# Gate chunks inside the last head of a differential attention, on one core

## The chip, the cores and the metric

One Trainium2 chip, one core of it. The metric is the device time in microseconds (us) of one execution. The kernel before takes 3123.36 us, the median of three runs (3120.61 to 3126.15).

## The reference

Two blocks one after the other on x of shape 1024 (sequence) x 1024 (channels), f32. The first has a short-convolution layer and a stick-breaking attention, and ends with an RMS norm. The change lies in the second block, which is, shortened:

```
h = rmsnorm_2(x, g_mix)
z = h @ w_in                              # u_pool, q, k, v
y_pool = pool_mixer(u_pool, w_pool_grp, pool_scale)
y_attn = diff_attention(q, k, v, ...)     # 8 heads, two score maps of depth 64 each
gates  = sigmoid(h @ w_gate + b_gate)     # 2048 columns
merged = gates[:, :1024] * (y_pool @ w_branch_pool)
       + gates[:, 1024:] * (y_attn @ w_branch_attn)
x = x + merged @ w_out
x = x + square(relu(rmsnorm_2(x, g_ffn) @ w_up)) @ w_down
```

In `diff_attention` a head's queries and keys are RMS-normalised, biased by distance and softmaxed in two maps; the head's output is (p0 - lambda p1) @ v, RMS-normalised over its 128 columns and scaled.

## The kernel before, in words

Everything is held transposed: channels on the 128 partitions, the 1024 positions along the free axis, in KT = 8 tiles. A **chunk** is one 128-column block of a weight matrix (128 x 1024 f32, 512 KB) times the whole operand: eight **steps**, one for each k tile (`step`, L549, through `mm3`, L541). To keep f32 precision each factor is split in a high part (rounded to fp32r) and a low part (the rest), and a step is three products, high x high, high x low, low x high, over two halves of 512 columns: six matmuls. The operand lies in HH and HL, the weights in WH[2] and WL[2], two slots used in turn.

The 215 chunks are numbered once for the whole program (C_AIN, C_AOUT, ..., C_GA, C_GRP, C_GP, C_QKV2, C_AB, C_WO, C_FF). Each goes through the same relay: SyncE (SP) loads it into the single buffer WR0 when chunk c-1 is fully split (`load_w`, waits on w_lo); ScalarE writes WH when chunk c-2 has been multiplied (`split_w`, L979, waits on chunk_done); GpSimd writes WL = WR0 - WH (L1828, w_lo). So a load, two splits and eight steps follow each other for each chunk, and SP's queue, which takes its instructions strictly in order, sets the order of all transfers.

PSUM is used as four pairs of banks of 1024 columns. Chunks before the second attention use pairs 0 and 1 in turn, by the parity of their number; free[p] counts how often pair p was emptied, and a chunk waits for it. USED gives the count at the start of each stage.

The stages around the change, in order:

- **Gate stage** (C_GA, 8 chunks): h @ w_gate for the attention half. ScalarE evicts each through Sigmoid into T[2] (L1208), SP stores it in g_a in HBM (L478), and ScalarE waits for that store.
- **Group chunk** (C_GRP) and **pool-gate stage** (C_GP, 16 chunks): the pool branch, multiplied by its gates (DVE, L1678), stored in m_p (L484); x is stored in x_d (L486).
- **Differential attention** (C_QKV2, 24 chunks: q, k, v of each head). The head's projections are always made on pair 0. Before the first head, three chunks stand alone. `attention_d` (L854 on TensorE, L1275 on ScalarE, L1712 on DVE) goes through eight slots s for the eight query blocks. Slot s makes the scores of block s (pairs 1 and 2), turns the weights of block s-1 (transposes into bank TB, L866), and for every second block makes the values (`value_sum`, L661, into bank OB). In heads 0 to 6, `steps` puts the 24 steps of the next head's three chunks between them, D_STEPS[s] in slot s, and `group_sums` (L829) adds up squares for the norms of the next queries and keys. DVE subtracts the bias and takes the row minimum (L1703), ScalarE takes exp (L1304, L1307), DVE combines the two maps (L1757, L1392). Each turned group goes PSUM to ATH on ScalarE (L1286) and to ATL on DVE (L1396); the next transposes into TB wait for that.
- **The last head** (j = 7, `fill=False`) has no next projections. The output stage's operand, the eight heads' outputs, is brought back instead: SP loads heads 0 to 5 from y_d into STGab (`operand_back`, L434), heads 6 and 7 are still in dOT. `operand_hi` (L1001, ScalarE) writes HH[k] and `operand_lo` (L1427, DVE) HL[k], one k in each slot from s = 2, and `next_chunk` (L665) gives TensorE one step of chunk C_AB behind it: k = 0 to 4 in slots 3 to 7, k = 5 and 6 behind the last turns. The eighth waits for the norm of the last head's output: copy (L1732), Square (L1345), `output_sums` (L840), Ln and Exp with a table load each (L1246, L1255), `norm_d` (L1389), then `operand_hi` and `operand_lo` for k = 7.
- **Output stage** (C_AB, 8 chunks). The loop over n: DVE multiplies the chunk by its gate, T[n % 2] (L1798), which frees the pair, adds the pool part, T[2 + n % 2] (L1800), and both parts are written to GH and GL. SP, once the last norm is done (d_n), reloads X from x_d (eight loads of 512 KB, L517), then weights, then for each n a gate from g_a (L523) and a pool part from m_p (L524). The T buffers lie over the attention's, so the first gate load also waits until HL is complete (f_lo).
- **C_WO and C_FF**: the projection back and the feed-forward part.

The lines of SP around the end of the last head:

```
            operand_back(y_d, "ab")
            sp.wait_ge(d_n, 3 * KT)
            for k in range(KT):
                sp.dma_start(kt(X, k), x_d[k]).then_inc(ld_xr, 16)
            load_w(C_AB + 2)
            sp.wait_ge(f_lo, FILL["ab"] + KT)
            for n in range(KT):
                if n >= 2:
                    sp.wait_ge(g_lo, KT + n - 1)
                sp.dma_start(T[n % 2], g_a[n]).then_inc(ab_ld[n % 2], 16)
                sp.dma_start(T[2 + n % 2], m_p[n]).then_inc(ab_ld[n % 2], 16)
```

Of the kernel before, what the change touches and what calls it, by code (L numbers as in the profile page):

```python
# [18 lines left out]
F32 = mybir.dt.float32  # L19
# [27 lines left out]
C_GRP = C_GA + KT  # L47
C_GP = C_GRP + 1
C_QKV2 = C_GP + 2 * KT
C_AB = C_QKV2 + 3 * KT  # L50
# [10 lines left out]
for _name, _w in (("mod_b", 64), ("a_g", 8), ("kv_g", 8), ("b_g", 8), ("conv", 24),  # L61
# [16 lines left out]
         ("bout", 4, 4, 0), ("pool", 2, 2, 0), ("ga", 4, 4, 0), ("gp", 8, 8, 0),  # L78
         ("qkv2", 24, 0, 0), ("ab", 4, 4, 0), ("wo", 4, 4, 0), ("ff", 32, 32, 0))
# [51 lines left out]

D_STEPS = (0, 2, 4, 2, 3, 5, 3, 5)
# [20 lines left out]
def block_kernel(nc, xt, cb, vecs, consts, mods, wst, out):  # L153
    with ExitStack() as ctx:
# [76 lines left out]

        raw_at = [[ATT + (2 * n + i) * 4 * S for i in range(2)] for n in (1, 3, 5)]
# [10 lines left out]
        OSUM = (S + HALF, 2 * S + HALF)  # L243
        TB = 3 * S
# [129 lines left out]
        ab_m = sem("ab_m")  # L374
        ff_r = sem("ff_r")
# [9 lines left out]
        def _(sp):  # L385
            def load_w(c):
                sp.wait_ge(w_lo, c)
                sp.dma_start(WR0[:, :], row(wst, c)).then_inc(ld_w, 16)
# [45 lines left out]
            def operand_back(src, name):  # L434
                for k in range(KT - 2):
# [37 lines left out]
            with sp.Fori(0, KT // 2) as i:  # L473
                for m in range(2):
                    s = (C_GA + m) % 2
                    load_w(2 * i + (C_GA + 2 + m))
                    sp.wait_ge(free[s], i + (USED["ga"][s] + 1))
                    sp.dma_start(row(g_a, 2 * i + m), T[2]).then_inc(ga_st, 16)  # L478
            load_w(C_GRP + 2)
            with sp.Fori(0, KT) as n:  # L480
                load_w(2 * n + (C_GP + 2))
                load_w(2 * n + (C_GP + 3))
# [5 lines left out]
            sp.wait_ge(ga_st, 16 * KT)  # L488
# [5 lines left out]
            for c in range(3):  # L494
                load_w(C_QKV2 + 2 + c)
# [5 lines left out]
            def attention_d(j, par, first=False):  # L501
                load_w(3 * j + (C_QKV2 + 5))
                if not first:
                    store_outputs(j - 1, 1 - par, 3 * j + 2)
                load_w(3 * j + (C_QKV2 + 6))
                load_w(3 * j + (C_QKV2 + 7))

            attention_d(0, 0, first=True)
            with sp.Fori(0, (KT - 2) // 2) as i:
                for m in range(2):  # L510
                    attention_d(2 * i + (1 + m), 1 - m)
            sp.wait_ge(d_s, 2 * ST * (KT - 1))
            sp.wait_ge(d_st, 16 * (KT - 2) + 16)
            operand_back(y_d, "ab")
# [25 lines left out]
        def _(pe):  # L540
# [262 lines left out]
            chunks("ga", C_GA, KT, HH, HL)  # L803
# [172 lines left out]
        def _(act):  # L976
# [298 lines left out]
            def attention_d(j, par, fill=True, first=False):  # L1275
# [13 lines left out]
                for s in range(ST):  # L1289
# [6 lines left out]
                    if not late:  # L1296
                        turned(s - 1, 1)
# [694 lines left out]
```

## Time and profile before

| What | Value |
|---|---|
| median of three runs | 3123.36 us |
| the profiled execution, its own time | 3123.29 us |
| its span, first to last instruction | 3121.5 us |
| mean granted TensorE clock | 0.964 |
| busy share of TensorE, DVE, ScalarE, GpSimd | 91%, 41%, 36%, 23% |

A row of the timeline gives the start in us from the span's start, the length in us, the engine (PE is TensorE, ACT is ScalarE, POOL is GpSimd, SPq is SyncE's queue), the line of the code, what is written from what, how often, and in brackets how long the engine stood idle before and what released it. A matmul is pipelined: two of 512 columns in one row last 0.62 us but start 0.46 us before the next two, so distances between starts are what counts. The granted clock is 1.00 at 2.4 GHz and 0.50 at 1.2 GHz.

### The profile page before, as it was taken

To read this page: it belongs to the slowest core of one execution; us is meant where nothing else is said; L and a number is where in the kernel's file an instruction comes from. 1 tells how busy PE (TensorE), PEld (TensorE's weight loads), DVE (VectorE), ACT (ScalarE), POOL (GpSimd) and SP (SyncE) were. 2 spreads that over 40 slices of the span, in tenths; PEclk is the share of its full clock that TensorE was granted. 3 is DMA by queue.
4 is the path that set the end of the run, shared out by engine and by line. 5 is a ranking of instruction groups with operands and counts; after the bars stand their busy time and mean duration, and the time that the engine had idled before them with its cause. 6 is when DMAs were issued, how large, how long until landed. Compare 5 with 4: busy or idle time off the path is not lost.

```text
span 3121.5 us, 38236 instructions
## 1 busy us (share of the span) xinstructions
PE 2855.8 (91%) x13672; PEld 2289.6 (73%) x13672; DVE 1268.7 (41%) x1815; ACT 1128.9 (36%) x1585; POOL 719.7 (23%) x387
## 2 busy tenths in 40 slices
PE   5999998998988875979998999998798999999999
PEld 3888886887777764758786767666586888888887
DVE  5544433125666654361102656556442412112121
ACT  3222213225566553233214666666312312112120
POOL 0222221223444431212232111110121122222222
PEclk8999999999999986989999999999899999999999
DMA  5333311442121120212231000001331111111112
GB/s 198 123 128 112 128 68 54 166 164 95 60 76 54 52 83 10 91 34 87 100 122 64 28 35 27 27 34 61 119 110 47 41 48 51 49 47 47 47 50 98
DMA packets 62571, 236.82 MB, mean 76 GB/s; under 512 B 6944, under 2 KB 7584, under 8 KB 59936
## 3 DMA queue, kind: packets, MB, share of 16 engines
q1 hardware_dynamic: 62496, 235.88, 21.2%
q8 instruction: 40, 0.66, 0.1%
q14 instruction: 35, 0.29, 0.0%
HBM read 191.81 MB, written 44.04 MB: 76 GB/s over the span
## 4 chain that ended last, share of the span: by engine, by line
issue 55%; PE 29%; DVE 6%; POOL 6%; ACT 3%; POOLq 0%; DVEq 0%; ACTq 0%; DMA 0%; SPq 0%
PE PS L545 19%; POOL WL L1828 6%; DVE bC L1581 2%; DVE ATL L1396 2%; PE PS L706 2%; PE PS L728 2%; PE PS L661 2%; ACT PS L1117 1%; PE PS L885 1%; PE PS L691 1%; PE PS L754 1%; PE PS L866 1%; PE PS L711 0%; ACT ATH L1286 0%; ACT bB L1116 0%
## 5 line engine op out<-in xcount | busy, mean ns | idle before, releaser
L1828 POOL TENSOR_TENSOR WL<-WR,WH 128x1024 fp32r<-128x1024 f32 x215 | 521.0, 2423 | 2085.6 <-ACT WH L984 1954.9
L545 PE MATMUL PS<-HH,WH 128*128 128x512 f32 x2272 | 727.6, 402 | 91.4 <-issue 28.9
L545 PE MATMUL PS<-HL,WH 128*128 128x512 f32 x2272 | 714.5, 396 | 0.0
L545 PE MATMUL PS<-HH,WL 128*128 128x512 f32 x2272 | 712.1, 395 | 0.0
L545 PEld LDWEIGHTS PS<-HH,WH 128*128 128x128 f32 x2272 | 426.9, 192 | 196.3 <-issue 72.9
L545 PEld LDWEIGHTS PS<-HL,WH 128*128 128x128 f32 x2272 | 435.7, 192 | 93.8
L545 PEld LDWEIGHTS PS<-HH,WL 128*128 128x128 f32 x2272 | 435.2, 192 | 93.5
L984 ACT ACTIVATE WH<-WR 128x1024 fp32r<-128x1024 f32 x214 | 225.7, 1055 | 589.6 <-PE PS L545 413.1
L545 PE MATMUL PS<-GH,WH 128*128 128x512 f32 x768 | 236.6, 389 | 1.5 <-DVE TMP L1798 1.5
L545 PE MATMUL PS<-GL,WH 128*128 128x512 f32 x768 | 236.5, 389 | 0.0
L545 PE MATMUL PS<-GH,WL 128*128 128x512 f32 x768 | 236.4, 389 | 0.0
L1581 DVE TENSOR_TENSOR_SCAN bC<-PS,EPSC 128x256 f32<-128x256 f32 (+7 forms) x128 | 172.9, 1352 | 102.6 <-ACT PS L1117 102.4
L1856 POOL TENSOR_TENSOR bB<-bB,bC 128x256 f32<-128x256 f32 (+7 forms) x128 | 154.0, 1205 | 177.0 <-DVE bC L1581 175.9
L1396 DVE TENSOR_TENSOR ATL<-PS,ATH 128x512 fp32r<-128x512 f32 (+3 forms) x288 | 152.6, 546 | 50.4 <-ACT ATH L1286 25.9
L545 PEld LDWEIGHTS PS<-GH,WH 128*128 128x128 f32 x768 | 144.0, 188 | 32.1 <-issue 1.9
L545 PEld LDWEIGHTS PS<-GH,WL 128*128 128x128 f32 x768 | 144.2, 188 | 30.0
L545 PEld LDWEIGHTS PS<-GL,WH 128*128 128x128 f32 x768 | 144.2, 188 | 29.9
L1820 DVE TENSOR_TENSOR X<-PS,X 128x1024 f32 x32 | 39.2, 1225 | 292.2 <-PE PS L545 292.2
L691 PE MATMUL PS<-IDF,bB 128*128 128x128 f32 x576 | 99.0, 298 | 58.1 <-DVE ATL L1396 57.4
L691 PEld LDWEIGHTS PS<-IDF,bB 128*128 128x128 f32 x576 | 67.2, 148 | 82.8 <-DVE ATL L1396 52.8
L1811 DVE SCALAR_TENSOR_TENSOR TMP<-PS,TMP 128x1024 f32<-128x1024 f32 x32 | 39.2, 1225 | 208.2 <-ACT TMP L1375 208.2
L1375 ACT ACTIVATE TMP<-PS 128x1024 f32<-128x1024 f32 x32 | 32.9, 1029 | 233.8 <-PE PS L545 233.8
(227 smaller groups left out, 3528.7 us busy)
## 6 DMA issues: line engine op xcount, KB each, us to landing
WR<-wst SPq DMA_DIRECT2D x215, 512.0 KB, 3.4
TMP<-mods SPq DMA_DIRECT2D x48, 512.0 KB, 3.5
MRAW<-mods SPq DMA_DIRECT2D x16, 512.0 KB, 11.0
v_hl<-VS SPq DMA_DIRECT2D x8, 1024.0 KB, 6.3
bV<-v_hl SPq DMA_DIRECT2D x8, 1024.0 KB, 7.6
X<-xt SPq DMA_DIRECT2D x4, 1024.0 KB, 8.1
x_b<-X SPq DMA_DIRECT2D x8, 512.0 KB, 4.8
k_hi<-KSH SPq DMA_DIRECT2D x8, 512.0 KB, 4.8
```

The source lines that it names most:

```text
L545: last = pe.matmul(PS[:, dst0 + q:dst0 + q + HALF], l, rr[:, k * S + q:k * S + q + HALF], start=a, stop=z)
L661: last = pe.matmul(PS[:, OB + (2 * n + r) * P:OB + (2 * n + 2) * P], v[:, kb * P:(kb + 1) * P], a[:, (2 * kb + r) * P:(2 * kb + 2) * P], s ...
L691: last = pe.transpose(PS[:, base + n * P:base + (n + 1) * P], bB[t % 2][h][:, kb * P:(kb + 1) * P], IDF[:, :])
L706: pe.matmul(PS[:, base + c0:base + c0 + w], l[par][rows, q], rr[par][rows, c0:c0 + w], start=i == 0, stop=i == 2 and c0 + w < n)
L728: last = pe.matmul(PS[:, o + r * P:o + 2 * P], value_weights(V, kb, h), a[:, (2 * kb + r) * P:(2 * kb + 2) * P], start=i == 0 and a is ATH ...
L984: act.activation(WH[slot][:, :], WR0[:, :], ACT.Identity).then_inc(w_hi, 1)
L1396: return dve.tensor_tensor(dst, value, high.bitcast(F32), ALU.subtract)
L1581: dve.tensor_tensor_scan(bC[h][:, S - n:S][:, ::-1], c, EPSC[:, 0:1].broadcast_to([P, n]), 1.0, ALU.mult, ALU.bypass).then_inc(free[1 + h], 1)
L1811: dve.scalar_tensor_tensor(out=T[2 + m], in0=PAIR[s], scalar=0.0, in1=T[m], op0=ALU.max, op1=ALU.mult).then_inc(free[s], 1)
L1820: dve.tensor_tensor(x, PAIR[s], x, ALU.add).then_inc(free[s], 1)
L1828: pool.tensor_tensor(WL[slot][:, :], WR0[:, :], WH[slot][:, :].bitcast(F32), ALU.subtract).then_inc(w_lo, 1)
L1856: pool.tensor_tensor(b, b, bC[h][:, S - n + 1:S + 1], ALU.mult).then_inc(b_a, 1)
```

## The change

Three of the eight gate chunks (C_GA2, GA_LATE = 3) leave the gate stage and come behind C_QKV2 in the numbering. The 24 steps are made in the last head, in the order D_LAST (steps ahead of and behind the second turn of each slot), on pair 0, as the projections are in the other heads. ScalarE evicts each without the sigmoid into a staging buffer GAS (`stage_gate`), SP stores it in g_a, and the sigmoid is taken in the output stage when the gate is back, for n = 5, 6, 7. The weights' order in HBM stays; `load_moved` maps the new numbers to the old places. HH and HL hold h until the 24 steps are done, so the operand of the output stage is written behind them: k = 0 ahead of the last turns, k = 1 behind them, 2 to 4 behind the Square, 5 and 6 behind Exp, all on DVE ahead of the last norm, then k = 7. TensorE makes both first output chunks step by step behind the last values, with the output sums after the third step, in pair 2 (OSUM_LAST). The gate stage's loops of SP and ScalarE are written out. On SP the weights of C_AB and C_AB+1 are loaded between the stores of the late gates, and those of C_AB+2 now ahead of the reloads of X.

The diff, cut to its core:

```diff
 C_GA = C_POOL + 4
-C_GRP = C_GA + KT
+GA_LATE = 3
+GA_FIRST = KT - GA_LATE
+C_GRP = C_GA + GA_FIRST
...
-C_AB = C_QKV2 + 3 * KT
+C_GA2 = C_QKV2 + 3 * KT
+C_AB = C_GA2 + GA_LATE
...
+D_LAST = ((0, 0), (2, 0), (2, 3), (0, 2), (2, 0), (2, 1), (2, 4), (2, 2))
...
+        GAS = [nc.alloc_sbuf_tensor_at(f"GAS{i}", [P, S], F32, offset=ATT + (8 + 2 * i) * 4 * S) for i in range(2)]
+        OSUM_LAST = (2 * S, 2 * S + HALF)
...
@@ SP, gate stage @@
+            for n in range(GA_FIRST):
+                s = (C_GA + n) % 2
+                load_moved(C_GA + 2 + n)
+                sp.wait_ge(free[s], n // 2 + (USED["ga"][s] + 1))
+                sp.dma_start(g_a[n], T[2]).then_inc(ga_st, 16)
...
@@ SP, last head @@
+            load_moved(C_GA2 + 2)
             sp.wait_ge(d_s, 2 * ST * (KT - 1))
             sp.wait_ge(d_st, 16 * (KT - 2) + 16)
-            operand_back(y_d, "ab")
+            operand_back(y_d, "ab", 0, 4)
+            for n in range(GA_LATE):
+                if n < 2:
+                    load_moved(C_AB + n)
+                sp.wait_ge(free[0], USED["ab"][0] - GA_LATE + n + 1)
+                sp.dma_start(g_a[GA_FIRST + n], GAS[n % 2][:, :]).then_inc(ga_late[n % 2], 16)
+            operand_back(y_d, "ab", 4)
+            load_w(C_AB + 2)
             sp.wait_ge(d_n, 3 * KT)
             for k in range(KT):
                 sp.dma_start(kt(X, k), x_d[k]).then_inc(ld_xr, 16)
-            load_w(C_AB + 2)
             sp.wait_ge(f_lo, FILL["ab"] + KT)
+            sp.wait_ge(ga_late[0], 32)
+            sp.wait_ge(ga_late[1], 16)
...
@@ TensorE, attention_d @@
                     early = 0 if s in (4, 6) else (D_STEPS[s] + 1) // 2
+                    late = D_STEPS[s] - early
+                    if not fill:
+                        early, late = D_LAST[s]
                     steps(early)
-                    if not fill and s >= 3:
-                        next_chunk(C_AB, C_AB % 2, "ab", s - 3)
                     turn(s - 1, 1)
                     values(s - 1)
-                    steps(D_STEPS[s] - early)
+                    steps(late)
                 if fill:
                     return
                 turn(ST - 1, 0)
-                next_chunk(C_AB, C_AB % 2, "ab", ST - 3)
                 turn(ST - 1, 1)
-                next_chunk(C_AB, C_AB % 2, "ab", ST - 2)
                 values(ST - 1)
                 pe.wait_ge(d_max, 2 * ST * KT)
-                output_sums(3 * KT)
+                pe.wait_ge(free[0], USED["ab"][0])
+                for kb in range(KT):
+                    if kb == 2:
+                        output_sums(3 * KT, OSUM_LAST)
+                    pe.wait_ge(f_lo, FILL["ab"] + kb + 1)
+                    step(C_AB, C_AB % 2, 0, HH, HL, kb)
+                    if 1 <= kb <= 5:
+                        step(C_AB + 1, (C_AB + 1) % 2, 1, HH, HL, kb - 1)
+                for kb in range(5, KT):
+                    step(C_AB + 1, (C_AB + 1) % 2, 1, HH, HL, kb)
...
@@ ScalarE, last head @@
+            def stage_gate(n):
+                act.wait_ge(chunk_done, C_GA2 + n + 2)
+                if n == 2:
+                    act.wait_ge(ga_late[0], 16)
+                act.activation(GAS[n % 2][:, :], PAIR[0], ACT.Identity).then_inc(free[0], 1)
...
                     if not late:
                         turned(s - 1, 1)
+                    if not fill and s == 3:
+                        stage_gate(0)
+                    if not fill and s == 6:
+                        stage_gate(1)
+                        split_w(C_AB, C_AB % 2)
...
                     if not fill:
-                        if s >= 2:
-                            operand_hi("ab", s - 2, dOT)
-                        if s == ST - 1:
-                            operand_hi("ab", KT - 2, dOT)
+                        if s == 3:
+                            split_w(C_GA2 + 2, (C_GA2 + 2) % 2)
                         continue
...
                 if not fill:
+                    stage_gate(2)
+                    operand_hi("ab", 0, dOT)
+                    split_w(C_AB + 1, (C_AB + 1) % 2)
                     turned(ST - 1, 0)
                     turned(ST - 1, 1)
+                    operand_hi("ab", 1, dOT)
                     act.wait_ge(d_o, ST // 2 * KT)
                     act.wait_ge(d_rs, 3 * KT - 1)
                     act.activation(dSQ[:, :], dOT[par][:, :], ACT.Square).then_inc(d_sq, 1)
-                    ln_outputs(3 * KT)
+                    for k in range(2, 5):
+                        operand_hi("ab", k, dOT)
+                    ln_outputs(3 * KT, OSUM_LAST)
                     exp_d(3 * KT, d_lo, KT)
+                    for k in range(5, KT - 1):
+                        operand_hi("ab", k, dOT)
                     act.wait_ge(d_n, 3 * KT)
                     operand_hi("ab", KT - 1, dOT)
...
@@ ScalarE, output stage @@
                     split_w(c + 2, c % 2)
+                if n >= GA_FIRST:
+                    act.wait_ge(ab_ld[n % 2], 32 * (n // 2 + 1))
+                    act.activation(T[n % 2], T[n % 2], ACT.Sigmoid, bias=vec("b_gate", 8 + n)).then_inc(ab_sg, 1)
                 act.wait_ge(ab_m, n + 1)
...
@@ DVE, last head @@
-                        if s >= 2:
-                            operand_lo("ab", s - 2, dOT)
-                        if s == ST - 1:
-                            operand_lo("ab", KT - 2, dOT)
                         continue
...
                 if not fill:
+                    operand_lo("ab", 0, dOT)
                     turned(ST - 1, 0)
                     turned(ST - 1, 1)
+                    operand_lo("ab", 1, dOT)
                     outputs(ST - 1)
+                    for k in range(2, KT - 1):
+                        operand_lo("ab", k, dOT)
                     norm_d(dOT[par], GS8[:, 0:1], 3 * KT)
                     operand_lo("ab", KT - 1, dOT)
...
@@ DVE, output stage @@
                 dve.wait_ge(ab_ld[n % 2], 32 * (n // 2 + 1))
+                if n >= GA_FIRST:
+                    dve.wait_ge(ab_sg, n - GA_FIRST + 1)
                 dve.tensor_tensor(gate, PAIR[s], gate, ALU.mult).then_inc(free[s], 1)
```

## Rows read from the trace of the kernel before

**Rows 1.** The page, part 1: busy us, share of the span, instructions.
```profile
PE 2855.8 (91%) x13672; PEld 2289.6 (73%) x13672; DVE 1268.7 (41%) x1815; ACT 1128.9 (36%) x1585; POOL 719.7 (23%) x387
```

**Rows 2.** Stretches: length, busy us per engine, granted clock, DMA share, GB/s.
```profile
2087.30:2153.80 66.50, 61.64 (x334) 45.87 (x334) 40.60 (x102) 43.87 (x69) 9.85 (x4) 1.00 0.18 63
2153.80:2161.40 7.60, 5.68 (x47) 4.96 (x46) 2.97 (x12) 3.90 (x8) 0.00 (x0) 1.00 0.01 2
2153.80:2229.10 75.30, 47.82 (x259) 35.06 (x258) 47.73 (x110) 41.90 (x69) 0.24 (x1) 0.86 0.06 20
2208.30:2214.30 6.00, 5.96 (x18) 4.69 (x19) 3.23 (x4) 1.20 (x2) 0.00 (x0) 0.50 0.00 0
2229.10:2235.00 5.90, 5.85 (x14) 4.59 (x15) 0.00 (x0) 0.00 (x0) 2.22 (x1) 0.50 0.93 358
```

**Rows 3.** Timeline, TensorE: start, us, instruction, xcount, idle before, releaser.
```profile
2208.34 1.08 PE L866 MATMUL PS<-IDF,dP 128*128 128x128 f32 x4 [2.57 <-DVE ATL L1396]
...
2229.15 1.22 PE L545 MATMUL PS<-HH,WH 128*128 128x512 f32 x2 [7.39 <-DVE HL L1396]
...
2246.14 0.70 PE L545 MATMUL PS<-HH,WH 128*128 128x512 f32 x2 [1.69 <-DVE TMP L1798]
```

**Rows 4.** Timeline, ScalarE, tail of the last head.
```profile
2221.80 1.27 ACT L1246 ACTIVATE dSQ<-PS,EPSC 128x512 f32<-128x512 f32 x2 [0.83 <-PE PS L844]
2223.08 1.28 ACT L1255 ACT_TABLE_LOAD   x1
2224.37 1.06 ACT L1255 ACTIVATE dRS<-dSQ 128x1024 f32<-128x1024 f32 x1
2226.78 1.06 ACT L1007 ACTIVATE HH<-dOT 128x1024 fp32r<-128x1024 f32 x1 [1.35 <-DVE dOT L1389]
2227.74 1.04 ACT L984 ACTIVATE WH<-WR 128x1024 fp32r<-128x1024 f32 x1
```

**Rows 5.** Timeline, DVE, tail of the last head and output stage.
```profile
2225.46 1.28 DVE L1389 SCALAR_TENSOR_TENSOR dOT<-dOT,GS,dRS 128x1024 f32<-128x1024 f32 x1 [6.89 <-ACT dRS L1255]
...
2244.67 1.23 DVE L1798 TENSOR_TENSOR TMP<-PS,TMP 128x1024 f32<-128x1024 f32 x1 [15.58 <-DMA TMP<-m_p]
...
2302.12 3.43 DVE L1800 TENSOR_TENSOR TMP<-TMP,TMP 128x1024 f32<-128x1024 f32 x1
```

**Rows 6.** DMA, 2226 to 2245 (40 slices; then landing us); last, m_p at 2246.
```profile
GB/s 0 0 0 69 155 423 397 423 414 371 173 267 336 397 371 354 354 405 423 423 423 414 448 388 397 397 405 431 423 423 414 414 414 431 328 173 69 26 9 0
...
X<-x_d SPq DMA_DIRECT2D x8, 512.0 KB, 7.4
...
TMP<-m_p SPq DMA_DIRECT2D x1, 512.0 KB, 12.3
...
DMA to landing us min/median/max: 5.5/5.5/5.5
```

**Rows 7.** Timeline, ScalarE, gate stage.
```profile
1457.64 1.28 ACT L984 ACT_TABLE_LOAD   x1 [8.79 <-PE PS L545]
...
1490.30 1.06 ACT L984 ACTIVATE WH<-WR 128x1024 fp32r<-128x1024 f32 x1 [6.11 <-PE PS L545]
```

**Rows 8.** Timeline, handover to the head's projections: TensorE, then ScalarE.
```profile
1640.37 0.73 PE L545 MATMUL PS<-HH,WH 128*128 128x512 f32 x2 [1.32 <-DVE TMP L1678]
...
1649.97 1.06 ACT L984 ACTIVATE WH<-WR 128x1024 fp32r<-128x1024 f32 x1 [0.41 <-DVE NLAM L1689]
```

**Rows 9.** Timeline, TensorE, head 6.
```profile
2115.00 1.98 PE L829 MATMUL PS<-dSQ,dBD 128*128 128x512 f32 x4 [0.26 <-ACT dSQ L1236]
...
2117.16 0.39 PE L661 MATMUL PS<-ATH,dVH 128*128 128x256 f32 x1 [0.18 <-DVE ATL L1396]
...
2119.05 0.70 PE L545 MATMUL PS<-HH,WH 128*128 128x512 f32 x2 [0.22 <-ACT dSQ L1241]
...
2134.24 1.98 PE L829 MATMUL PS<-dSQ,dBD 128*128 128x512 f32 x4
...
2136.64 0.44 PE L866 MATMUL PS<-IDF,dP 128*128 128x128 f32 x2 [0.41 <-DVE ATL L1396]
```

More of the change, by code:

```diff
@@ L374, in block_kernel @@
         ab_m = sem("ab_m")
+        ab_sg = sem("ab_sg")
+        ga_late = [sem(f"ga_late{i}") for i in range(2)]
         ff_r = sem("ff_r")
@@ L385, in _, with load_w, load_moved @@
         def _(sp):
[L386 removed]
+            def load_w(c, at=None):
                 sp.wait_ge(w_lo, c)
[L388 removed]
+                sp.dma_start(WR0[:, :], row(wst, c if at is None else at)).then_inc(ld_w, 16)
+            def load_moved(c):
+                if isinstance(c, int) and C_GA2 <= c < C_AB:
+                    load_w(c, c - C_GA2 + C_GA + GA_FIRST)
+                elif isinstance(c, int) and (c < C_GRP or c >= C_AB):
+                    load_w(c)
+                else:
+                    load_w(c, c + GA_LATE)
             sp.dma_start(CB, cb).then_inc(ld_cb, 16)
@@ L433, in _, with operand_back @@
             sp.wait_ge(st_x, KT * 16)
-            def operand_back(src, name):
-                for k in range(KT - 2):
+            def operand_back(src, name, first=0, last=KT - 2):
+                for k in range(first, last):
                     if k >= 4:
@@ L472, in _ @@
                 load_w(c + (C_POOL + 2))
[L473 to L479, printed above, removed]
+            for n in range(GA_FIRST):
[3 more added lines that the diff above has]
+                sp.dma_start(g_a[n], T[2]).then_inc(ga_st, 16)
+            load_moved(C_GRP + 2)
             with sp.Fori(0, KT) as n:
-                load_w(2 * n + (C_GP + 2))
-                load_w(2 * n + (C_GP + 3))
+                load_moved(2 * n + (C_GP + 2))
+                load_moved(2 * n + (C_GP + 3))
                 sp.wait_ge(free[(C_GP + 1) % 2], n + (USED["gp"][(C_GP + 1) % 2] + 1))
@@ L802, in _ @@
                 chunk(C_POOL + g, s, s, uu[s] + 1)
-            chunks("ga", C_GA, KT, HH, HL)
+            chunks("ga", C_GA, GA_FIRST, HH, HL)
+            chunk(C_GRP - 1, (C_GRP - 1) % 2, (C_GRP - 1) % 2, GA_FIRST // 2 + USED["ga"][(C_GRP - 1) % 2])
             cg = C_GRP
@@ L906, in steps @@
                     nonlocal k
-                    for _ in range(n if fill else 0):
+                    for _ in range(n):
                         c = k // KT
@@ L1202, in _ @@
                 act.activation(kt(MXH, g), T[3], ACT.Identity).then_inc(p_mh, 1)
-            with act.Fori(0, KT // 2) as i:
-                for m in range(2):
-                    s = (C_GA + m) % 2
-                    act.wait_ge(chunk_done, 2 * i + (C_GA + m + 2))
-                    split_w(2 * i + (C_GA + m + 2), s)
-                    act.activation(T[2], PAIR[s], ACT.Sigmoid, bias=vec("b_gate", 2 * i + (8 + m))).then_inc(free[s], 1)
-                    act.wait_ge(ga_st, 32 * i + 16 * (m + 1))
+            for n in range(GA_FIRST):
+                s = (C_GA + n) % 2
+                act.wait_ge(chunk_done, C_GA + n + 2)
+                split_w(C_GA + n + 2, s)
+                act.activation(T[2], PAIR[s], ACT.Sigmoid, bias=vec("b_gate", 8 + n)).then_inc(free[s], 1)
+                act.wait_ge(ga_st, 16 * (n + 1))
             for g in range(4):
```

35 lines of the change are left out of this document (16 added, 19 removed).

## The prediction

> **What bounds the kernel now.** I read the page first: TensorE is busy in 91% of the span [rows 1], so a change pays only where TensorE waits, or where it moves work into a wait. Then the stretches around the last head [rows 2]. In each, the reader compares PE busy with the length, and reads the granted clock. Head 6 (they count from 0), from its first score to the first score of the last, takes 66.5 us, 61.6 of them busy, at clock 1.00: 24 matmul steps of the next head's projections fill it. The last head has only seven steps of the output stage's first chunk: 75.3 us to the eighth, 47.8 busy, clock 0.86. Against a chain of softmax work that 24 steps hardly lengthen elsewhere, some 27 us are idle, and this is the room for the change.
>
> What ends the head's waits is in [rows 3 to 5]. The eighth step starts at 2229.15 after 7.39 us for the last low part, behind the chain Ln, table load, Exp, norm, high part, low part. The first output-stage chunk that needs a PSUM pair back starts at 2246.14: it waits 1.69 us for the multiply at 2244.67, which itself waited 15.58 us for m_p. That load is late because eight reloads of X, 512 KB each, and one weight load stand ahead of it on SP's queue [rows 6]; the first may start only when the norm of the last output is done (2225.46 + 1.28 = 2226.74). m_p needed 12.3 us to land, against 5.5 with little ahead of it. So **two clocks run to 2246**: TensorE's, and norm plus 17.9 us of loads (2244.67 - 2226.74). They are nearly even now.
>
> I count from A, the last head's first score (2153.80, the end of head 6 in its stretch in [rows 2]). Before, the norm is done at A+72.9 and the third output chunk starts at A+92.3.
>
> **Removed ahead of the head: -32.7.** ScalarE takes up a gate chunk when TensorE has finished it; from 1457.64 to 1490.30 are three chunks of 10.9 us with no wait of TensorE between [rows 7]. Three go: 32.7 us. With them goes what each issued: a weight load, a split on ScalarE and one on GpSimd, a sigmoid, a store; all come back later. The group chunk behind the gates now waits for the last eviction at its first product instead of its second. The next wait is for that gate's store either way, so I take 0.
>
> **Handover to the head's projections: -0.6.** Three fewer chunks swap the pairs of the stage before. The 1.32 us wait at 1640.37 for the multiply to free pair 0 disappears, since the multiply now uses pair 1. But ScalarE's next split (1649.97) waits for the lambda chain, which stays [rows 8]. Bounds 0 and 1.3; half, as the split and not the chunk sets the next sum.
>
> **The last head, TensorE to the end of step 24: T = A+62.0.** It now carries 24 steps, as head 6 does, so I start from 66.5. Gone are two group sums of the projections, with what waits on them: 0.26 + 2.16 (2115.00 to 2117.16) + 0.18 and 0.22 around the values, and 2.40 (2134.24 to 2136.64): 5.2 [rows 9]. Gone is the next head's first score, 0.5. New are waits where the single pair 0 changes hands inside a slot. After the eighth step ScalarE must evict (1.06) before the ninth starts: +1.2. The second eviction hides behind the values. The third falls behind the head. The evictions stand ahead of the exponentials of slots 3 and 6, and delay them 1 and 2 us. DVE, the last turns and TensorE wait for those; but head 6 has table loads and a Ln at about those places (1.28 + 1.1 + 1.28 by the like in [rows 4]), and no turn is late there. The low parts of the operand, one for each slot, leave DVE. Sum 66.5 - 5.2 - 0.5 + 1.2 = 62.0. Bounds 60 and 66: below if the values' waits go too, above if the last turn, tied with step 24 (DVE's chain alone gives A+61.8 or so), comes late.
>
> **Behind T: the norm at T+26.1.** From a head's last turn to the end of its values takes 7.60 - 0.5 = 7.1 us [rows 2]. Here ScalarE does the third eviction, a high part and the split of the second output chunk first, 0.96 us apart each [rows 4]; 0.7 us of waiting is in the 7.1 already: +2.2. Two waits of TensorE, about 4 and 1.5 us, should take the clock to 1.2 GHz, as the 2.57 us before 2208.34 and the wait ahead of it did (0.50 for 6.0 us [rows 2, 3]): +2.3 on the values; 0 if it holds. So values end at T+11.6. Three steps follow (4.1, +0.4 for the clock), then the output sums, 1.9: T+18.0. Ln, table load, Exp up to the norm take 3.66 (2221.80 to 2225.46 [rows 4, 5]): T+21.7. But ScalarE and DVE have been given the parts 5 and 6 ahead of the norm: two high parts 1.9, the last low part 1.2, norm 1.3: T+26.1. The switch from Ln to Exp costs 1.28 in the row, with Exp 0.01 us behind it. The Trainium skill (ScalarE: Activation LUTs, What ACT_TABLE_LOAD costs) adds a drain of about 1.38 us to every switch. By it the forecast would be 1.4 us later; the row shows no drain and decides.
>
> **The third output chunk: A+106.3, against A+92.3.** The load of its weights now goes ahead of X's, so 512 KB less are queued: 0.524 MB at 423 GB/s is 1.2 us [rows 6]. Norm to multiply is 17.9 - 1.2 = 16.7, then 1.5 to TensorE's start. 62.0 + 26.1 + 16.7 + 1.5 = 106.3. TensorE is ready at T+12.0 (values, and the slow rest) + 16 steps of 1.36 (a chunk's 10.9 over eight) + 1.3 for the sums = T+35.1 = A+97.1. **So the expected gain of the fill is partly given back in a wait of 9.2 us for the gate loads.** Behind it the clock is down for 5.9 us, as at 2229.1 [rows 2]: 2.9 more. Head and handover cost 14.0 + 2.9 = +16.9.
>
> **Later gates: 0.** Chunks 5 to 7 take their sigmoid in the output stage. Their multiply comes some 2 us later, 3.4 once with a table load; but the add behind it took 3.43 us at 2302.12, against 1.23 for an operation of the same size at 2244.67 [rows 5]; it ran beside GpSimd's split, and a later one need not. TensorE wants the pair a chunk of 10.9 us later. The last sigmoid can run before its chunk ends, once the loads are there. Bound +1.5, if it can't.
>
> **Sum.** -32.7 - 0.6 + 16.9 = -16.4. The profiled execution took 3123.29 us (span 3121.5), the median is 3123.36, so they are the same to 0.1: **3107 us**. The case's own range is 3101 to 3113: no fall of the clock ahead of the values takes 2.3 off, T ends -2 and +4, the last gate +1.5.
>
> **Rivals.**
> - *The gate loads don't wait for X's.* They are issued about 4.4 us behind the norm and land 5.5 later, as the second m_p did [rows 6]. The multiply is at A+98.1, the chunk at A+99.6, the wait 2.5 us: 3123.3 - 33.3 + 7.3 = 3097; 3094 if the clock holds too. Against it: the first m_p took 12.3 us with the same loads ahead. The Trainium skill (DMA: Bandwidth & Descriptors, Queues, rings and completion order) says a later transfer may finish before an earlier one, though rings are consumed in order; by that this rival has its chance, and the trace does not show it.
> - *Half hidden.* The last head's chain takes the evictions and splits badly, T comes 10 to 22 us late, and the time is within 6 us of before.
> - *In series: slower.* Place: the softmax chain of slots 3 to 7, where TensorE reaches a turn only after steps that sit behind ScalarE's evictions. Before, the last turn started at A+54.5, with five steps ahead of it, 8.4 us of that (one at half clock: 2.7 + 4 x 1.4). If all 24 came on top: 46.1 + 32.8 = A+78.9 at full clock, over A+100 with most at 1.2 GHz. It decides from T = A+84.7 on (16.4 + 6.3 later), so with at least four steps at half clock; with all of them slow, about 3150. Against it: head 6 hides the same 24.
>
> **How the numbers follow.** What a measurement of this kernel can tell from no change is 0.2%, or 6.2 us. Forecast 0.75, loads free 0.13, half hidden 0.07, in series 0.05. The first two are faster: 0.88; same 0.07; slower 0.05. The range reaches to the loads rival's low end and past the forecast's high one: 3093 to 3114.
>
> **What would show it.** In the profile of the changed kernel: five sigmoids in the gate stage, and the head's first score 33 us earlier; 24 steps to A+62 at clock near 1.00; about 4 us of waiting between the last two turns; the norm at A+88; after the second output chunk a wait of 9 us that ends on the multiply, and that on m_p, with clock 0.50 behind it. I am wrong if the multiply comes within 3 us of the second chunk's end, if a turn in the head waits over 2 us, or if the output stage's later chunks wait for sigmoids.

## The result and the profile after

The changed kernel takes **3104.2 us** (median of five runs, 3103.5 to 3112.4) against 3122.3 of the kernel before beside it (five runs, 3120.6 to 3126.2): ratio 0.9947, with an interval of 0.9933 to 0.9962, so 18.1 us less by the medians. (The ratio comes from the single runs, so it isn't quite the quotient of the medians.) Two executions among the runs below, one of 5719.6 us in r1 and one of 13154.6 us of the kernel before beside r9, lie far outside all others and are in none of the figures given. The forecast was 3107. The profiled execution took 3104.21 us, its span is 3102.4; with 3123.29 of the one before, the two traces differ by 19.1 us, and it is this sum that they have to explain.

The page, part 1, of the changed kernel, beside [rows 1]:

```profile
PE 2848.9 (92%) x13672; PEld 2286.0 (74%) x13672; DVE 1265.2 (41%) x1815; ACT 1123.1 (36%) x1582; POOL 720.9 (23%) x387
```

The matmuls are the same 13672. TensorE was idle for 3121.5 - 2855.8 = 265.7 us before and is for 3102.4 - 2848.9 = 253.5 now. The rest, 6.9 us, is in the busy time itself, which depends on the clock.

Stretches of the changed kernel, columns as in [rows 2]: head 6; the last head to the end of its 24 steps; its last values; the wait of the third output chunk; what follows it; the start of C_WO; and the whole from A (now 2115.03) to that chunk:

```profile
2048.50:2115.00 66.50, 61.63 (x333) 45.85 (x332) 40.62 (x102) 43.84 (x69) 9.84 (x4) 1.00 0.09 32
2115.00:2177.20 62.20, 57.31 (x325) 44.47 (x325) 36.60 (x98) 30.79 (x57) 7.28 (x3) 1.00 0.23 77
2181.70:2187.50 5.80, 4.29 (x21) 4.09 (x22) 1.92 (x2) 1.54 (x2) 1.15 (x1) 0.57 0.46 142
2213.00:2221.00 8.00, 0.00 (x0) 0.00 (x0) 1.35 (x2) 0.00 (x0) 0.00 (x0) 0.73 1.03 420
2221.10:2226.90 5.80, 5.80 (x14) 4.54 (x15) 4.64 (x4) 2.00 (x2) 2.46 (x1) 0.50 0.15 61
2291.60:2297.60 6.00, 6.00 (x20) 4.76 (x21) 3.09 (x3) 2.00 (x2) 2.50 (x1) 0.72 0.00 0
2115.00:2221.10 106.10, 87.66 (x458) 69.32 (x457) 50.59 (x112) 48.55 (x76) 12.11 (x5) 0.95 0.35 126
```

The same stretch of the kernel before, from A to its last turn:

```profile
2153.80:2208.34 54.54, 36.10 (x212) 26.30 (x211) 41.38 (x104) 32.76 (x59) 0.00 (x0) 0.90 0.06 20
```

The last head now looks like head 6: 57 of 62 us busy at clock 1.00 up to its last turn, where it was 36 of 55 at 0.90. The fourth row of the changed kernel is the price: 8 us in which TensorE does nothing while the DMA engines move 420 GB/s.

TensorE's timeline, beside [rows 3]: the pair handed over inside slot 3, the two last turns, the values, the third output chunk, and the first chunk of C_WO:

```profile
2141.77 0.73 PE L572 MATMUL PS<-HH,WH 128*128 128x512 f32 x2 [1.11 <-ACT GAS L1312]
...
2177.22 0.60 PE L894 MATMUL PS<-IDF,dP 128*128 128x128 f32 x4
2181.69 0.63 PE L894 MATMUL PS<-IDF,dP 128*128 128x128 f32 x4 [3.87 <-DVE ATL L1447]
2183.82 0.55 PE L688 MATMUL PS<-ATH,dVH 128*128 128x256 f32 x1 [1.50 <-DVE ATL L1447]
...
2221.08 1.19 PE L572 MATMUL PS<-HH,WH 128*128 128x512 f32 x2 [8.18 <-DVE TMP L1851]
...
2291.56 1.05 PE L572 MATMUL PS<-GH,WH 128*128 128x512 f32 x2 [2.20 <-DVE TMP L1851]
```

DVE, beside [rows 5]: the last norm, the first gate, the last gate:

```profile
2202.11 1.28 DVE L1440 SCALAR_TENSOR_TENSOR dOT<-dOT,GS,dRS 128x1024 f32<-128x1024 f32 x1
...
2219.61 1.22 DVE L1851 TENSOR_TENSOR TMP<-PS,TMP 128x1024 f32<-128x1024 f32 x1 [13.87 <-DMA TMP<-m_p]
...
2290.07 1.23 DVE L1851 TENSOR_TENSOR TMP<-PS,TMP 128x1024 f32<-128x1024 f32 x1 [4.40 <-ACT TMP L1412]
```

ScalarE, beside [rows 4, 7]: its take-up at the gate stage's end, which was at 1490.30; the last gate's eviction, a high part, a weight split and, behind these three, the eviction of the last turns' first half; Ln's result, table load and Exp; and the last sigmoid:

```profile
1456.37 1.06 ACT L1017 ACTIVATE WH<-WR 128x1024 fp32r<-128x1024 f32 x1 [8.81 <-PE PS L572]
...
2177.42 1.02 ACT L1312 ACTIVATE GAS<-PS 128x1024 f32<-128x1024 f32 x1 [2.28 <-PE PS L572]
2178.34 1.05 ACT L1040 ACTIVATE HH<-STGab 128x1024 fp32r<-128x1024 f32 x1
2179.28 1.05 ACT L1017 ACTIVATE WH<-WR 128x1024 fp32r<-128x1024 f32 x1
2180.23 0.59 ACT L1325 ACTIVATE ATH<-PS 128x512 fp32r<-128x512 f32 x1
...
2196.50 1.28 ACT L1287 ACT_TABLE_LOAD   x1
2197.79 1.06 ACT L1287 ACTIVATE dRS<-dSQ 128x1024 f32<-128x1024 f32 x1
...
2288.78 1.15 ACT L1412 ACTIVATE TMP<-TMP,VEC 128x1024 f32<-128x1024 f32 x1 [4.38 <-DMA TMP<-m_p]
```

And the transfers issued from 2203 to 2222, beside [rows 6] (KB each, median us from issue to landing; g_a and m_p are two loads each, and the first of them took 10.7 and 11.2):

```profile
X<-x_d SPq DMA_DIRECT2D x8, 512.0 KB, 7.5
TMP<-g_a SPq DMA_DIRECT2D x2, 512.0 KB, 9.9
TMP<-m_p SPq DMA_DIRECT2D x2, 512.0 KB, 10.6
```

### The profile page after: what moved, and what is told of

It reads as the page before. It is cut to its first block, busy times and chain, and to the rows that moved or that the text cites. A ratio compares the mean times of both kernels' runs of the same rounds, so it can differ in the third digit from the quotient of the medians.

```text
span 3102.4 us, 38102 instructions
## 1 busy us (share of the span) xinstructions
PE 2848.9 (92%) x13672; PEld 2286.0 (74%) x13672; DVE 1265.2 (41%) x1815; ACT 1123.1 (36%) x1582; POOL 720.9 (23%) x387
## 4 chain that ended last, share of the span: by engine, by line
issue 56%; PE 27%; DVE 6%; POOL 6%; ACT 3%; POOLq 0%; DMA 0%; DVEq 0%; ACTq 0%; SPq 0%
PE PS L572 17%; POOL WL L1881 6%; DVE bC L1632 2%; DVE ATL L1447 2%; PE PS L733 2%; PE PS L755 2%; PE PS L688 2%; ACT PS L1150 1%; PE PS L913 1%; PE PS L718 1%; PE PS L781 1%; PE PS L894 1%; PE PS L738 0%; ACT ATH L1325 0%; ACT bB L1149 0%
## 5 line engine op out<-in xcount | busy, mean ns | idle before, releaser
L572 PEld LDWEIGHTS PS<-HL,WH 128*128 128x128 f32 x2272 | 434.4, 191 | 93.3
```

What stands on the lines that cost most here:

```text
L572: last = pe.matmul(PS[:, dst0 + q:dst0 + q + HALF], l, rr[:, k * S + q:k * S + q + HALF], start=a, stop=z)
```

## The experiments

All were run in three batches on three chips, each with runs of the kernel before beside it (medians 3123.9, 3123.5 and 3124.1 us over 17, 17 and 16 runs; r12 was run alone on a fourth, beside 3126.4). Marks are counted from A, the last head's first score. In that count the changed kernel has: last turn 62.2, norm done 88.4, third output chunk 106.1 after a wait of 8.2.

**r1, the changed kernel again**, for its marks on another chip.

> The changed kernel once more, as the measure for the other runs beside it. 3104 us, within 4. If the 1.2 us by which its profile was ahead of the one before already at 1338 us, where the code is the same, is a matter of the single execution, the two profiles there differ by another amount in this run.

Measured: 3100.1 (the median of four runs, 3094.9 to 3105.2), ratio 0.9917 [0.9902, 0.9931]. Last turn at 62.2, norm at 88.4, third chunk at 105.5 after 7.6. So the marks inside the head and tail repeat to 0.6 us, and the whole time doesn't: it spreads over 10 us. The last section comes back to that. At 1338 us, where the code is the same, this profile is 0.5 us ahead of the one before, and not 1.2: over all the traces here the sums at that place start between 1332.2 and 1339.5. The 1.2 us are a matter of the single execution.

**r2, the first gate loads ahead of X's.** Nothing else is changed:

```diff
             load_w(C_AB + 2)
+            sp.wait_ge(f_lo, FILL["ab"] + KT - 2)
+            sp.dma_start(T[0], g_a[0]).then_inc(ab_ld[0], 16)
+            sp.dma_start(T[2], m_p[0]).then_inc(ab_ld[0], 16)
             sp.wait_ge(d_n, 3 * KT)
...
-                sp.dma_start(T[n % 2], g_a[n]).then_inc(ab_ld[n % 2], 16)
-                sp.dma_start(T[2 + n % 2], m_p[n]).then_inc(ab_ld[n % 2], 16)
+                if n:
+                    sp.dma_start(T[n % 2], g_a[n]).then_inc(ab_ld[n % 2], 16)
+                    sp.dma_start(T[2 + n % 2], m_p[n]).then_inc(ab_ld[n % 2], 16)
```

> The first gate and pool part are loaded ahead of the eight reloads of X, as soon as six low parts of the operand are written. Theory (queue): the 8.2 us wait of TensorE ahead of the third output chunk is for loads that stand behind 4 MB of X; it goes to under 1 us, the third chunk starts at A+98 instead of A+106.1, the clock stays at 1.00 behind it (2.9 us more), total 11 us less than the changed kernel, about 3093. Rival (bandwidth or order only moved): the second gate's loads come behind X instead, TensorE waits ahead of the fourth chunk, and under 4 us are gained: 3100 to 3104.

Measured: **3093.6** (3090.7 to 3096.4), ratio 0.9901 [0.9887, 0.9915]. The stretch from 2190 to 2214 of this kernel, then its DVE in the timeline (A is 2116.41):

```profile
2190.00:2214.00 24.00, 24.00 (x104) 19.16 (x104) 12.93 (x10) 12.82 (x13) 2.39 (x1) 1.00 0.51 187
```

```profile
2209.73 1.22 DVE L1855 TENSOR_TENSOR TMP<-PS,TMP 128x1024 f32<-128x1024 f32 x1 [3.12 <-PE PS L576]
...
2221.69 1.22 DVE L1855 TENSOR_TENSOR TMP<-PS,TMP 128x1024 f32<-128x1024 f32 x1 [4.91 <-DMA TMP<-m_p]
```

TensorE runs through, 24.00 of 24.00 us at clock 1.00, and the first gate's multiply waits for TensorE, at A+93.3 and not at A+104.6. The second one does wait for its m_p, but its chunk is long enough to cover that. From A to C_WO it is 164.7 us against 176.5: 11.8 less, of which the wait is 8.2 and the clock behind it 2.9, as forecast. Against r1's trace (174.5) it is 9.8 less. So the queue was the cause, and the wait costs 10 to 12 us in all in the traces. The times say it less sharply: 10.6 us below the changed kernel, but 6.5 below r1 beside it, and r2's interval overlaps r1's.

**r3, the last turns ahead of most of that work**: on ScalarE the first of them ahead of the gate's eviction and both ahead of the high part and the weight split, and on DVE both ahead of the first low part (ScalarE's part of the edit):

```diff
-                    stage_gate(2)
-                    operand_hi("ab", 0, dOT)
-                    split_w(C_AB + 1, (C_AB + 1) % 2)
                     turned(ST - 1, 0)
+                    stage_gate(2)
                     turned(ST - 1, 1)
+                    operand_hi("ab", 0, dOT)
+                    split_w(C_AB + 1, (C_AB + 1) % 2)
                     operand_hi("ab", 1, dOT)
```

> ScalarE takes the evictions of the last turns ahead of the last gate's eviction, the first high part and the weight split. Theory (what stands ahead on ScalarE, and the clock that falls for it): the 3.87 us wait between the last two turns goes to under 1 us, the values run at clock 1.00 and end at T+7.4 instead of T+11.8, the norm comes at T+21.7 instead of T+26.2, the third output chunk 4.5 us earlier: about 3099.5. Rival (the wait is the bank's, for DVE's low part, and the clock falls in any case): under 1.5 us gained, 3103.

Measured: 3102.1 (3099.0 to 3104.8), ratio 0.9928 [0.9915, 0.9941]. TensorE's timeline and the stretch of the values:

```profile
2181.63 0.63 PE L894 MATMUL PS<-IDF,dP 128*128 128x128 f32 x4 [1.50 <-DVE ATL L1447]
2183.76 0.55 PE L688 MATMUL PS<-ATH,dVH 128*128 128x256 f32 x1 [1.50 <-DVE ATL L1447]
```

```profile
2183.76:2188.80 5.04, 5.04 (x24) 5.04 (x24) 3.88 (x2) 1.96 (x3) 2.47 (x1) 0.50 0.30 106
```

The first wait falls from 3.87 to 1.50, so the work put ahead of the last turns was its cause, and the norm comes 2.0 us earlier. Most of that is ScalarE's three operations, though the run moved DVE's low part too: in the changed kernel DVE was done with it at 2180.65, and still waited 0.20 us for ScalarE. But the values still run at clock 0.50 behind two waits of 1.50: the clock term, which I had tied to the long wait, isn't won back. The third chunk comes only 0.9 to 1.5 us earlier (A+104.6), and the time isn't below r1's. The wait's half of this expectation held, the clock's and the time's didn't.

**r4, the new tail without the fill**: all eight gate chunks back in the gate stage, the last head empty, the output stage's operand still written behind it.

```diff
-GA_LATE = 3
+GA_LATE = 0
-D_LAST = ((0, 0), (2, 0), (2, 3), (0, 2), (2, 0), (2, 1), (2, 4), (2, 2))
+D_LAST = ((0, 0),) * 8
```

> All eight gate chunks back in the gate stage, no steps in the last head, the rest of the new tail kept. Theory (the steps fill waits): without 24 steps the last head's chain still takes 44 to 50 us to its last turn instead of 62, so 12 to 18 of the 32.7 us come back: 3104 + 32.7 - 15 = 3122, 3118 to 3126. Rival (in series): the last turn comes at A+30, the gain of the gate stage and the length of the head cancel: 3104 within 3.

Measured: 3129.1 (twelve runs, 3120.0 to 3133.1), ratio 1.0014 [1.0005, 1.0022]. The last head of this kernel, from A to its last turn, and its third output chunk:

```profile
2152.97:2209.21 56.24, 35.10 (x182) 25.69 (x181) 36.33 (x99) 27.88 (x54) 2.39 (x1) 0.72 0.00 1
```

```profile
2251.42 1.19 PE L564 MATMUL PS<-HH,WH 128*128 128x512 f32 x2 [8.39 <-DVE TMP L1833]
```

This splits the change in two. Writing the operand behind the head costs by itself: the third chunk stands at A+98.4 and not at A+92.3, 6.1 us later, and the whole is 5.3 us slower than before. The 24 steps then lengthen A to the third chunk from 98.4 to 105.5 or 106.1, by 7.1 to 7.6 us, and relieve the gate stage of 32.7: 25 to 26 us net, and 3129.1 less the changed kernel's 3104.2 or r1's 3100.1 is 25 or 29.

The expectation missed: 3129.1 lies above its 3118 to 3126. My number for the head was wrong. Empty, it takes 56.2 us to the last turn, at clock 0.72; the kernel before, with five steps in it, takes 54.5, at 0.90. So a head without the steps is no shorter, and taking their time off, as I did here and in the prediction's "in series" rival (54.5 - 8.4 = 46.1), was the error.

**r5, the last norm two operations earlier** on DVE:

```diff
-                    for k in range(2, KT - 1):
+                    for k in range(2, 5):
                         operand_lo("ab", k, dOT)
                     norm_d(dOT[par], GS8[:, 0:1], 3 * KT)
-                    operand_lo("ab", KT - 1, dOT)
+                    for k in range(5, KT):
+                        operand_lo("ab", k, dOT)
```

> DVE makes the last norm ahead of the low parts 5 and 6. Theory (two clocks: the third output chunk starts norm plus 17.9 us of loads): the norm comes 3.3 us earlier (2202.1 minus 2198.8 in the changed kernel's profile), X's reloads, the gate's load and the third chunk as well: 3101, with a wait of 5 instead of 8.2 us. Rival (the loads are bound by the last low part or by the weights, not by the norm): no change, 3104.

Measured: 3098.4 (3096.7 to 3099.7), ratio 0.9919 [0.9906, 0.9932]. The third chunk in the timeline (A is 2112.19):

```profile
2214.69 1.19 PE L572 MATMUL PS<-HH,WH 128*128 128x512 f32 x2 [4.58 <-DVE TMP L1852]
```

The norm is 3.2 us earlier (85.2), the chunk 3.0 to 3.6 (102.5 against 105.5 and 106.1). So the run of loads that starts with the norm is what counts here, and an operation ahead of the norm moves the third chunk by its length. In the times it isn't to be seen: the ratio is r1's.

**r6, the kernel before with its first gate loads ahead of X's**, the edit of r2.

> The kernel before with the first gate's loads ahead of X's. Theory (in the kernel before the loads and TensorE were nearly even, so the same repair brings only the 1.69 us wait): 1 to 2.5 us less than before, 3120 to 3121. Rival (the loads cost both kernels alike): 8 us or more less, 3114.

Measured: 3122.8, ratio 0.9999 [0.9991, 1.0008]: nothing. Two rows, TensorE and ScalarE:

```profile
2245.97 0.70 PE L550 MATMUL PS<-HH,WH 128*128 128x512 f32 x2 [1.56 <-POOL WL L1833]
```

```profile
2242.32 1.06 ACT L989 ACTIVATE WH<-WR 128x1024 fp32r<-128x1024 f32 x1 [13.40 <-DMA WR<-wst]
```

I had expected 1 to 2.5 us, and that missed. The multiply comes at A+78.6, 12 us earlier than before, and the third chunk at A+92.33, as before (A+92.34). In the kernel before, the chunk's weights also stand behind X. Their low part was ready at 2245.72 (GpSimd, 2243.35 + 2.37), 0.2 us ahead of the gate's multiply (2244.67 + 1.23), so it took over as the last wait. Only the changed kernel loads the weights ahead of X, and only there is the gate load alone last.

**r7, the edits of r2, r3 and r5 together; r8, these and one step moved** from slot 3 to slot 4; **r9, r7 with a semaphore of its own for the g_a loads**, so that the late sigmoid doesn't wait for m_p too; **r11, r7 again.** The edit of r9:

```diff
-                    act.wait_ge(ab_ld[n % 2], 32 * (n // 2 + 1))
+                    act.wait_ge(ab_ga[n % 2], 16 * (n // 2 + 1))
                     act.activation(T[n % 2], T[n % 2], ACT.Sigmoid, bias=vec("b_gate", 8 + n)).then_inc(ab_sg, 1)
```

> Loads first, norm first and turns first together. Theory: with the loads first the norm no longer sets the third chunk, so the sum is 11 from the loads and 4.4 from the turns and their clock, and nothing from the norm: 3104 - 15.4 = 3089. Rival (the parts cover each other, the last low part of the operand becomes the bound): 3093, no better than the loads alone.

> As the one with all three, and the ninth step moved from slot 3 to slot 4, so that the first gate's eviction lies under the scores. Theory: the 1.11 us wait for pair 0 goes, and the last turn comes 1.1 us earlier: 3088. Rival (the last turn is tied with DVE's chain of the last slot, so a step earlier brings nothing): 3089.

> All three repairs, and the gates' loads count on a semaphore of their own, so that the late sigmoids wait for the gate alone and not for the pool part behind it. Theory (the last sigmoid comes late because of the pool part's load, and the wait it makes ahead of the projection back costs clock as well): that wait goes from 2.1 to 2.8 us back to 1.5 as in the kernel before, the stretch from there to the next sums from 92.9 back to 91.3 us: 2.3 less than with the three, about 3090. Rival (the wait is set elsewhere): no change, 3092.

> All three once more beside the one with its own semaphore. 3092 within 3; the spread of the single executions comes from the seven heads, each 66.5 or 68.0 us long by whether the clock falls once in it.

| Kernel | median us | ratio | C_WO's first wait | C_WO to the sums behind it |
|---|---|---|---|---|
| r7 | 3092.3 | 0.9898 [0.9884, 0.9912] | 2.77 | 92.89 |
| r11 | 3093.7 | 0.9906 [0.9892, 0.9921] | 2.02 | 91.25 |
| r8 | 3090.2 | 0.9892 [0.9878, 0.9905] | 2.21 | 92.89 |
| r9 | 3090.2 | 0.9886 [0.9870, 0.9901] | 1.50 | 91.26 |

Together the three edits are hardly worth more than r2 alone (3093.6): once TensorE doesn't wait for the gate, an earlier norm frees nothing. So r7's rival held. r8's moved step took the 1.11 us wait away, as expected, but a turn then waits 2.59 us for DVE (A+30.9), and the last two turns come 2.8 us later than in r7 (A+65.0 against 62.2) and not 1.1 earlier; TensorE still doesn't wait ahead of the third chunk, and the time shows no difference. r9 takes a term away in the trace: its TensorE, its ScalarE and the stretch behind C_WO's start:

```profile
2284.16 0.70 PE L577 MATMUL PS<-GH,WH 128*128 128x512 f32 x2 [1.50 <-DVE TMP L1858]
```

```profile
2281.10 1.15 ACT L1417 ACTIVATE TMP<-TMP,VEC 128x1024 f32<-128x1024 f32 x1 [3.39 <-DMA TMP<-g_a]
```

```profile
2284.20:2290.20 6.00, 6.00 (x27) 4.96 (x28) 3.11 (x3) 2.01 (x2) 2.49 (x1) 1.00 0.00 0
```

The sigmoid now waits for g_a alone. The changed kernel waits 2.20 before C_WO, has the clock at 0.72 in the next 6 us and takes 92.9 us to the sums. r9, like the kernel before, waits 1.50, keeps 1.00 and takes 91.3. The clock's part, 1.6 us, isn't certain to come: it is there in the changed kernel, r2, r3, r5, r7 and r8 with waits of 2.06 to 2.77 us, and not in r11 with 2.02, nor in r1, the changed kernel itself, with 2.11 (91.3 us to the sums). So what r9 shows is the wait, 0.7 us; that it also keeps the clock isn't shown. In the runs' times r7, r8, r9 and r11 can't be told apart. By the medians all lie below both kernels, and r9 has the lowest ratio, the only one whose interval is clear of r1's: 34 us below the kernel before and 10 to 14 below the changed one.

**r10 and r12, the kernel before with the gate stage's loops written out** on SP and ScalarE, as the change does by the way.

```diff
-            with sp.Fori(0, KT // 2) as i:
-                for m in range(2):
...
+            for n in range(KT):
+                s = (C_GA + n) % 2
+                load_w(C_GA + 2 + n)
+                sp.wait_ge(free[s], n // 2 + (USED["ga"][s] + 1))
+                sp.dma_start(g_a[n], T[2]).then_inc(ga_st, 16)
```

> The kernel before with nothing but the gate stage's two loops (SP and ScalarE) written out. Theory (what the changed kernel gains ahead of the last head beyond the three chunks comes from the swapped pairs and the clock they meet): no change against before, 3123 within 1.5. Rival (it comes from the loops: two table loads each round): the group chunk and the stage behind it come 1 to 3 us earlier, 3120 to 3122.

> The kernel before with the gate stage's loops written out, for another profile. The last one's executions lay in two groups, 3110 to 3116 and 3121 to 3126, and the profiled one was in the upper. Theory (clock): if this profiled execution falls in the lower group, the difference lies in the seven heads, more of them 66.5 instead of 68.0 us long, or at the starts of stages, and the last head and the tail are the same to 0.5 us. Rival (the loops save work): the gate and group stages are shorter by 7 us or more. If it falls in the upper group, it stays open.

Measured: r10 3115.8 (twelve runs in two groups, 3109.9 to 3115.8 and 3121.1 to 3125.9), ratio 0.9977 [0.9965, 0.9989]; r12 3123.0 (eight runs, 3110.3 to 3125.9), 0.9982 [0.9967, 0.9997]. Both profiled executions fell in the upper group, and r10's has the stages where the kernel before has them (the pool-gate stage starts at 1505.39 against 1505.33, A is 2152.11 against 2153.80). Where they differ, no trace shows. But both intervals lie below 1, by some 7 and 6 us, and none of r6's twelve executions, with the loops as they were, is as short as the lower group. So the loops written out may have a part in the changed kernel's gain, and it stays open how large. r4 against r1 isn't touched by this, as both have them.

## Why the prediction was right

The mechanism held, with its price. That the sum came as near as it did is in part luck: the gain ahead of the head was 5.5 us larger than forecast, and 3.1 us more than forecast were lost behind the third chunk.

In the table, the first four rows are differences of start times between the two traces, the rest is counted from A or T as in the prediction.

| Step | Forecast | In the trace |
|---|---|---|
| three gate chunks | -32.7 | 1490.30 to 1456.37: -33.9, of which -1.2 was there at 1338 (1338.03, now 1336.83), where the code is the same |
| group chunk | 0 | pool-gate stage 1505.33, now 1470.30: -35.0, so -1.1 |
| handover | -0.6 | first group sum 1653.68, now 1616.05: -37.6, so -2.6 |
| A | -33.3 | -38.8 |
| T | A+62.0 | A+62.2, clock 1.00 |
| wait for pair 0 | 1.2 | 1.11 |
| waits between the last turns | 4 and 1.5 | 3.87 and 1.50 |
| end of the values | T+11.6 | T+11.8 |
| norm done | A+88.1 | A+88.4 |
| third output chunk | A+106.3, wait 9.2 | A+106.05, wait 8.18 |
| clock behind it | 5.9 us at half | 5.8 us at 0.50 |
| later gates | 0, bound +1.5 | +2.3 (0.7 of waiting, 1.6 of clock) |
| sum | -16.4 | -19.1 |

**What held.** The head and its tail, from A to the third output chunk, came out within 0.3 us at every mark (the third chunk by two small misses against each other: the norm 0.3 us late, the loads behind it 16.2 us and not 16.7), and r2 to r5 each showed one of its causes: the fill (r4) is worth 25 to 26 us; the gate loads wait behind X (r2); the norm starts that clock (r5); the order of the work ahead of the last turns makes the 3.87 (r3). The wait ahead of the third chunk was 1.0 us shorter than forecast, mostly as TensorE was ready at A+97.9 and not at A+97.1, which cost nothing. The cost of the table switch is also as forecast: the load at 2196.50 lasts 1.28 us and Exp follows at 2197.79. By the drain that the Trainium skill (ScalarE: Activation LUTs, What ACT_TABLE_LOAD costs) adds, the norm would have come at A+89.5; it came at A+88.4, so the trace doesn't agree.

**The rivals.** That the gate loads don't wait for X's (3097) fell: the first multiply is at A+104.6, not A+98.1. SP issued g_a and m_p 4.1 and 4.9 us behind the first X, and the multiply started 11.3 us after m_p's issue (2208.32 to 2219.61), though DVE was long free. The loads landed in the order of the queue here (m_p at 2219.5, the weights behind it at 2220.8, the next g_a at 2222.0), which agrees with what the Trainium skill (DMA: Bandwidth & Descriptors, Queues, rings and completion order) says of rings consumed in order. Half hidden and in series fell as well: the last turn came at A+62.2, where they needed 72 and 84.7.

**What was off: the sizes of two groups of terms, against each other.**

*Ahead of A the gain was 5.5 us larger* (38.8 against 33.3). The mis-sized terms were the zero at the group chunk and the 0.6 at the handover: I looked for waits there and had no term for TensorE's clock, nor one for the loops written out (r10, r12). The 5.5 are 1.2 that were there at 1338, ahead of any changed line, and differ from execution to execution (r1); 1.1 and 2.6 less 0.6 around the pool-gate stage; and 1.1 in the stages up to A. For the middle part the traces have a witness, r3, whose code up to there is the changed kernel's. The first 5 us of the pool-gate stage, in the changed kernel and then in r3:

```profile
1470.30:1475.30 5.00, 5.00 (x22) 4.17 (x23) 0.00 (x0) 0.00 (x0) 1.65 (x1) 1.00 0.34 103
```

```profile
1474.00:1479.00 5.00, 4.97 (x12) 3.94 (x13) 0.00 (x0) 0.00 (x0) 1.65 (x1) 0.50 0.36 104
```

The kernel before has 0.50 there too. Counted from 1338's sums, the stage starts 167.3 us on before, 134.6 in r3 (32.7 less, the forecast) and 133.5 in the changed kernel. From there to the first group sum it is 148.4, 148.8 and 145.8. So the 3 us around the first group sum are the clock's level at this place, which the same code has one way or the other: 1.00 in the traces of the changed kernel, r1, r2, r5, r8 and r9, 0.50 in r3, between them in r7 and r11. They aren't a wait that went. At the same level, r3 takes 0.4 us longer here than the kernel before, so the 0.6 us that I gave the handover don't show. What sets the level in a given execution is open. The traces of the kernel before, r6 and r10 have 0.50 here and r12's has 0.69, so the change may make the higher level likelier; no run shows it.

*Behind the third chunk 3 us more were lost* (from 25.1 ahead to 19.1, where 2.9 were forecast). "Later gates: 0, bound +1.5" was the wrong step. I wrote that the last sigmoid can run before its chunk ends, once the loads are there. But it ran at 2288.78, after 4.38 us for a load, and its semaphore counts g_a and m_p together; so C_WO waited 2.20 and not 1.50, and behind that the clock fell to 0.72: 2.3 in all, over my bound. The prediction names "if the output stage's later chunks wait for sigmoids" as a sign of being wrong, and the last one's multiply did, by 4.40 us. r9 took the wait away; the clock's 1.6 us came in this execution and not in r1's. Another 0.8 is between the sums and the feed-forward's first chunk (10.67 us against 9.87); that stretch takes from 9.7 to 11.1 us in the other traces, and 11.07 in r10's and r12's of the kernel before, so it isn't the change's. The argument for the earlier late gates was right: DVE's add lasts 1.23 us behind a late sigmoid (2272.64) and 3.43 beside GpSimd's split (2247.14).

## What to carry to other kernels

Work put into a hole under a latency chain is nearly free (24 steps of 1.36 us made this head 6 us longer than r4's empty one and 8 us longer than before), but then the chain's successors become the bound: ask which loads are tied to the end of that chain, and in what order they stand on their queue. Two loads of 512 KB ahead of eight others, a matter of four lines, were worth another 10 to 12 us in the traces, and nothing in the kernel before (r6), where a second load stood in the same place: a wait has to be last before its removal pays. A semaphore that counts two loads makes the one that needs only the first wait for both.

## What the hardware showed that I had not expected

**The clock falls after short waits, and not always.** In r3 two waits of 1.50 us were enough for 0.50 in the values. In the heads ahead of the last, with the same instructions, some run at 1.00 throughout and some don't. SP's store of a head's output marks its length; two heads of the changed kernel in one execution, then the two stretches:

```profile
1869.52 0.36 SPq L515 DMA_DIRECT2D y_d<-dOT  x1
...
1937.51 0.36 SPq L515 DMA_DIRECT2D y_d<-dOT  x1
...
2003.94 0.35 SPq L515 DMA_DIRECT2D y_d<-dOT  x1
```

```profile
1869.50:1937.50 68.00, 63.14 (x336) 47.25 (x332) 40.71 (x102) 43.84 (x69) 9.82 (x4) 0.97 0.09 31
1937.50:2003.90 66.40, 61.51 (x334) 45.83 (x332) 40.51 (x102) 43.85 (x69) 9.85 (x4) 1.00 0.09 32
```

The difference, 1.6 us, is TensorE's busy time, at 0.97 against 1.00. How many heads are of the one or the other kind changes from execution to execution: the five heads between these stores take 4 x 66.5 and one of 68.0 in r5's trace and five times 68.1 in r1's. The stretch from the first transposes of v (1649.55 in the changed kernel) to A, the same code in all, took from 461.3 to 469.3 us in the traces of these kernels. A difference of 3 us between two of these kernels is therefore no more than hinted at by four or five runs.

**A load waits for what is ahead of it in its queue.** One core drew 420 GB/s on the mean through the whole wait (the fourth stretch above); behind eight loads of 512 KB, the first g_a and m_p landed 10.7 and 11.2 us after their issue, against 5.5 for the second m_p in [rows 6] with little ahead.
